# A two-layer decoder step: raw inputs to the projections, gates and cached values in another order

## What is computed

```
xn = x * rsqrt(mean(x*x) + eps) * norm_attn            # the factor rsqrt(...) is one number per token
u, q, k, v, gates = split(xn @ w_in)                   # 512 + 3*1536 + 2048 columns
q, k = rmsnorm per head of q, k
pool_o = mixer of running means of u;  att_o = three attention groups, prompt and cached keys and values
x += (sigmoid(g0) * (pool_o @ w_bp) + sigmoid(g1) * (att_o @ w_ba)) @ w_out
x += FFN(rmsnorm(x))           # layer 0: dense SwiGLU; layer 1: top 2 of 8 experts
```

## Time and profile before

| what | value |
|---|---|
| median of three runs | 1980.35 us |
| the profiled execution itself | 1980.97 us |
| its span, first to last instruction | 1979.2 us |
| TensorE busy | 1900.2 us (96%) |
| VectorE, ScalarE, POOL busy | 621.4, 466.5, 165.1 us |
| mean granted TensorE clock | 0.985 |
| moved by DMA | 553.81 MB, 280 GB/s |

### The profile page before, as it was taken

How to read it: one execution, slowest core, us unless ns; L and a number is a source line. 1 busy time by engine, 2 the same in 40 slices (tenths; PEclk the granted TensorE clock), 3 DMA queues, 4 the chain that set the end, 5 groups by cost and what they waited for, 6 DMA issues and landing times.

```text
span 1979.2 us, 44750 instructions
## 1 busy us (share of the span) xinstructions
PE 1900.2 (96%) x20521; PEld 1305.5 (66%) x20522; DVE 621.4 (31%) x1037; ACT 466.5 (24%) x708; POOL 165.1 (8%) x239
## 2 busy tenths in 40 slices
PE   6999988999999999998899999999999999999998
PEld 5998876999999999886786353443535353443534
DVE  4455631554444445641353101020101102020101
ACT  3444432344433444532232100000000000000000
POOL 0113100113321011400010000000000000000000
PEclk8999999999999999999998999999999999999999
DMA  7443688745545444388935999999999999999996
GB/s 235 158 143 126 216 281 303 244 129 170 169 162 169 136 151 153 124 277 275 312 103 191 350 408 380 412 374 416 387 403 406 382 409 379 412 375 415 393 398 267
DMA packets 211901, 553.81 MB, mean 280 GB/s; under 512 B 11402, under 2 KB 107706, under 8 KB 195056
## 3 DMA queue, kind: packets, MB, share of 16 engines
q1 hardware_dynamic: 207184, 541.67, 74.1%
q0 software_dynamic: 3248, 9.18, 1.3%
q10 hardware_dynamic: 1280, 0.06, 0.1%
HBM read 543.46 MB, written 7.77 MB: 279 GB/s over the span
## 4 chain that ended last, share of the span: by engine, by line
PE 91%; DMA 3%; DVE 3%; ACT 2%; issue 1%; POOL 0%; SPq 0%; DVEq 0%; ACTq 0%; POOLq 0%
PE psum L906 86%; PE psum L914 5%; DMA low_part<-in_w_in 3%; DVE w_split L1739 1%; ACT w_split L1470 1%; DMA high_part<-in_const_a 0%; DVE high_part L1746 0%; DVE low_part L2201 0%; DVE low_part L1732 0%; DVE low_part L1834 0%; ACT high_part L1447 0%; DVE high_part L1839 0%; ACT low_part L1443 0%; POOL high_part L2357 0%; DVE high_part L1732 0%
## 5 line engine op out<-in xcount | busy, mean ns | idle before, releaser
L906 PE MATMUL psum<-low_part 128*32 128x512 f32 (+3 forms) x6926 | 672.0, 526 | 6.8 <-ACT low_part L1443 4.7
L906 PE MATMUL psum<-xn_split,w_split 128*128 128x288 f32 x3744 | 530.3, 302 | 37.7 <-DVE w_split L1739 21.9
L906 PEld LDWEIGHTS psum<-xn_split,w_split 128*128 128x128 f32 x3744 | 515.3, 193 | 62.8 <-DVE w_split L1739 35.4
L906 PEld LDWEIGHTS psum<-low_part 128*32 128x32 f32 (+2 forms) x6926 | 241.4, 114 | 405.1 <-issue 397.3
L1739 DVE TENSOR_TENSOR w_split<-low_part,w_split 128x2048 fp32r<-128x2048 f32 x105 | 240.9, 2294 | 367.6 <-ACT w_split L1470 367.5
L906 PE MATMUL psum<-low_part,high_part 128*32 128x256 f32 (+3 forms) x6636 | 345.1, 359 | 3.9 <-DVE low_part L1732 2.4
L906 PEld LDWEIGHTS psum<-low_part,high_part 128*32 128x32 f32 (+1 forms) x6636 | 218.5, 111 | 130.0 <-issue 15.6
L1470 ACT ACTIVATE w_split<-low_part 128x2048 fp32r<-128x2048 f32 x105 | 200.9, 1914 | 366.7 <-PE psum L906 230.8
L2213 DVE TENSOR_TENSOR low_part<-high_part,psum 128x384 f32<-128x384 f32 (+1 forms) x48 | 29.8, 621 | 426.2 <-PE psum L906 423.8
L914 PE MATMUL psum<-high_part,low_part 128*128 128x128 f32 (+2 forms) x839 | 107.7, 278 | 12.5 <-DMA high_part<-in_const_a 9.4
L1703 ACT ACTIVATE high_part<-psum 128x384 f32<-128x384 f32 (+1 forms) x48 | 25.9, 544 | 395.0 <-PE psum L906 394.1
(11 more groups left out here) (153 smaller groups left out, 919.5 us busy)
## 6 DMA issues: line engine op xcount, KB each, us to landing
low_part<-in_we_down SPq DMA_DIRECT2D x112, 1024.0 KB, 8.4
low_part<-in_cache_kv_g SPq DMA_DIRECT2D x72, 1024.0 KB, 5.6
low_part<-in_we_gate SPq DMA_DIRECT2D x64, 1024.0 KB, 8.0
low_part<-in_we_up SPq DMA_DIRECT2D x64, 1024.0 KB, 8.4
low_part<-in_w_in SPq DMA_DIRECT2D x56, 1024.0 KB, 5.1
low_part<-in_we_gate SPq DMA_DIRECT2D x64, 768.0 KB, 7.4
low_part<-in_we_up SPq DMA_DIRECT2D x64, 768.0 KB, 6.8
low_part<-in_w_dense SPq DMA_DIRECT2D x33, 1024.0 KB, 5.2
```

Of the source, the lines that this page charges most:

```text
L906: signal(e.matmul(out, lhsT, rhs, start=start, stop=stop, skip_group_check=mixed), inc)
```

## The change

- **Factor behind the projections.** In both layers the attention norm's projections take raw x times the gain: ScalarE makes its high part (`raw_high`), VectorE its low part (`raw_low`). `rstd` is multiplied when u, v and gate tiles are evicted, on VectorE now; q and k need it only in the epsilon of their own norm, for which VectorE adds eps * rms^2 to the sums (head sums). v tiles and gates were evicted on ScalarE before; ScalarE now takes the sigmoid from SBUF.
- **Squares.** POOL adds the eight squared tiles, and one sum-of-squares product with ones remains per norm. It stands after the second z tile (attention), or after the first FFN tile.
- **Start.** SP sends the identity, then the inputs and the first weight chunk in halves, chunks 1 to 4, and then the rest of the table. Transposes, copies, splits and the first two u tiles go by halves of the features.
- **Layer 1's start.** The last FFN chunk runs column by column, its sums in banks 4 to 7 and 0 to 3; VectorE makes a low part after each column that it adds.
- **FFN.** Its second chunk is split ahead of root and reciprocal.
- **Gate stage.** Value chunks follow each half of a gate chunk, and gates 1 to 7 are loaded one value chunk earlier than they are used (`value_loads`). The second head gather comes after the last gate, and the first two pool branch tiles before the attention ones (`branch_tiles`).
- **Evictions.** v tiles are evicted ahead of the weight split of the same step on VectorE.

```
-V_BEHIND = (2, 3, 3, 3, 3, 2, 2, 0)
+V_BEHIND = ((1, 1), (1, 1), (2, 1), (1, 1), (2, 1), (1, 1), (1, 1), (2, 0))
 
 
 def value_steps():
 
     out, v = [], 0
-    for gate, n in enumerate(V_BEHIND):
-        out.append(("G", gate))
-        out += [("V", v + i) for i in range(n)]
-        v += n
+    for gate, behind in enumerate(V_BEHIND):
+        for x, n in enumerate(behind):
+            out.append(("G", gate, x))
+            out += [("V", v + i, 0) for i in range(n)]
+            v += n
     return out
 
 
 V_STEPS = value_steps()
 
 
+def value_loads():
+
+    out = [(kind, n) for kind, n, x in V_STEPS if x == 0]
+    for gate in range(1, KT):
+        i = out.index(("G", gate))
+        if out[i - 1][0] == "V":
+            out[i - 1], out[i] = out[i], out[i - 1]
+    return out
+
+
+V_LOADS = value_loads()
...
+    js = [(("x", tt, 0), None) for tt in range(3)] + [(("gain", 0), None)]
+    return js + [(("x", tt, 1), None) for tt in range(3)]
...
-    js = [(("ssq", 0), None)]
-    js += [(("u", c), None) for c in range(PG)]
+    js = [(("u", c), (4, 5, 6, 7)) for c in range(PG)]
     for n in range(36):
+        if n == 2:
+            js.append((("ssq", 0), (3,)))
...
-    return js + [(("fd", c), None) for c in range(KT)]
+    return js + [(("fd", c), ((c + 4) % KT,)) for c in range(KT)]
...
+            e.dma_start(ident, io["const_a"][:, 0:PART]).then_inc(ident_loaded, 16)
+            def columns(w, a):
+                return w.rearrange("(k p) n -> p k n", p=PART)[:, :, a:a + 256]
+
+            for hf in range(2):
+                for tt, (a, n) in enumerate(TT):
+                    src = io["x_prompt"][0, a:a + n, :] if tt < 2 else io["x_sample"].rearrange("b t d -> (b t) d")
+                    half = slice(D // 2 * hf, D // 2 * (hf + 1))
+                    e.dma_start(x_raw[0:n, tt, half], src[:, half]).then_inc(x_loaded[hf], 16)
+                k = slice(KT // 2 * hf, KT // 2 * (hf + 1))
+                e.dma_start(view(slot(0), KT, 256)[:, k], columns(io["w_in"][0], 0)[:, k])\
+                    .then_inc(loaded[0] if hf else half_loaded, 16)
...
-                for kind, n in V_STEPS:
+                for kind, n in V_LOADS:
...
-                for k in range(KT):
-                    e.wait_ge(sq_ready.sem, sq_ready.at(L, 8 * i + k + 1))
-                    mm(S.ps(("ssq", i))[:, 0:T], ones, work[:, k, :], k == 0, k == KT - 1,
-                       full[S.bank(("ssq", i))] if k == KT - 1 else None)
-
-            def ssq_tile(L, S, k):
-
-                if k == 0:
-                    S.wait_free(e, ("ssq", 1))
-                e.wait_ge(sq_ready.sem, sq_ready.at(L, 8 + k + 1))
-                mm(S.ps(("ssq", 1))[:, 0:T], ones, work[:, k, :], k == 0, k == KT - 1,
-                   full[S.bank(("ssq", 1))] if k == KT - 1 else None)
+                e.wait_ge(sq_sum.sem, sq_sum.at(L, (KT - 1) * (i + 1)))
+                mm(S.ps(("ssq", i))[:, 0:T], ones, work[:, 0, :], True, True, full[S.bank(("ssq", i))])
...
+            for hf in range(2):
+                e.wait_ge(x_loaded[hf], 48)
...
+                    w = held.rearrange("p a (k n) -> p a k n", k=KT)
+                    for h in range(2):
+                        if (L, h) == (0, 1):
+                            e.wait_ge(lo_ready, 1)
+                        for c in range(2):
+                            job = ("u", c)
+                            if h == 0:
+                                S.wait_free(e, job)
+                            for k in range(KT // 2 * h, KT // 2 * (h + 1)):
+                                if c == 0:
+                                    e.wait_ge(xl_ready.sem, xl_ready.at(L, k + 1))
+                                mm3(S.ps(job)[:, 0:T], [w[:, a, k, 128 * c:128 * (c + 1)] for a in range(2)],
+                                    [x[:, k, :] for x in xn_parts], k == 0, k == KT - 1,
+                                    full[S.bank(job)] if k == KT - 1 else None)
+                    done.append(split_used)
...
+                    if n == 2:
+                        ssq(L, S, 0)
...
-                def gates(n):
+                def gates(n, x):
                     w = chunk(L, W_MERGE + n).rearrange("p a (k n) -> p a k n", k=KT)
-                    for x in range(2):
-                        project(S, (f"g{n % 2}", n // 2 * 2 + x), lambda a, k: w[:, a, k, 128 * x:128 * (x + 1)], xn_parts)
-                        if (n, x) == (KT - 1, 0):
-                            gather_heads(1)
-                    done.append(split_used)
-
-                for kind, n in V_STEPS:
+                    project(S, (f"g{n % 2}", n // 2 * 2 + x), lambda a, k: w[:, a, k, 128 * x:128 * (x + 1)], xn_parts)
+                    if x == 1:
+                        done.append(split_used)
...
+                for kind, n, x in V_STEPS:
                     if kind == "V":
                         cache_values(n)
                         continue
-                    gates(n)
-                    if n == 0:
+                    gates(n, x)
+                    if (n, x) == (0, 1):
                         turn_s_probs(1)
-                    elif n == EX0_GATE:
+                    elif (n, x) == (EX0_GATE, 1):
                         gather_heads(0)
+                    elif (n, x) == (KT - 1, 1):
+                        gather_heads(1)
...
-                    if c >= 1 and L == 0:
-                        ssq_tile(0, dense_sec, c - 1)
...
-                                ssq_tile(0, S, KT - 1)
+                                ssq(0, S, 1)
...
+                    if i < FT // 2 - 1:
+                        for f in (2 * i, 2 * i + 1):
+                            e.wait_ge(hl_ready, f + 1)
+                            for n in range(KT):
+                                down(w, f, n)
+                    else:
+                        e.wait_ge(hl_ready, FT)
+                        for n in range(KT):
+                            for f in (2 * i, 2 * i + 1):
...
+            def raw_high(L, k):
+
+                e.activation(xn_split[:, 0, k, :], xT[:, k, :], ACT.Copy, scale=gain[:, k:k + 1]).then_inc(xh_ready.sem, 1)
...
+                        turned_x(1, hf)
+                        if hf == 1:
+                            turned_x(2, 1)
+                        first_halves(hf)
+                        for tt in range(3):
+                            pre.wait_read(e, ("x", tt, hf))
+                        if hf == 0:
+                            e.wait_ge(gain_ready.sem, gain_ready.at(0, 1))
+                        for k in range(4 * hf, 4 * hf + 4):
+                            raw_high(0, k)
+                else:
+                    e.wait_ge(gain_ready.sem, gain_ready.at(1, 1))
+                    for k in range(KT):
+                        dense_sec.wait_read(e, ("fd", k))
+                        raw_high(1, k)
+                split_high(L, 1)
+                for k in range(KT):
+                    e.activation(work[:, k, :], xT[:, k, :], ACT.Square).then_inc(sq_ready.sem, 1)
+                split_high(L, 2)
+                split_high(L, 3)
+                root(S, 0)
...
-                    elif c >= 24:
-                        v = c - 24
-                        copy(S, ("zv", v), vT[v // 4][:, v % 4, :], S.ps(("zv", v))[:, 0:T])
...
-                        S.freed(e.activation(gate[2 * job[1] + n % 2], S.ps(job)[:, 0:T], ACT.Sigmoid), job)
-                        if (n, x) == (KT - 1, 0):
+                        g = gate[2 * job[1] + n % 2]
+                        e.wait_ge(gate_scaled.sem, gate_scaled.at(L, 2 * n + x + 1))
+                        e.activation(g, g, ACT.Sigmoid).then_inc(gate_ready.sem, 1)
...
-                norm(0, S, 1, W_UP + 1)
+                split_high(0, W_UP + 1)
+                root(S, 1)
...
-                for k in range(KT + 1 if i == 0 else 0):
-                    if k < KT:
-                        e.scalar_tensor_tensor(out=xn[:, k, :], in0=xT[:, k, :], scalar=gain[:, 8 * i + k:8 * i + k + 1],
-                                               in1=rstd, op0=ALU.mult, op1=ALU.mult).then_inc(xn_ready.sem, 1)
-                    if k >= 1:
-                        e.wait_ge(xh_ready.sem, xh_ready.at(L, 8 * i + k))
-                        e.tensor_tensor(xn_split[:, 1, k - 1, :], xn[:, k - 1, :], xn_split[:, 0, k - 1, :].bitcast(F32),
-                                        ALU.subtract).then_inc(xl_ready.sem, 1)
...
+            def raw_low(L, i, k):
+
+                e.wait_ge(xh_ready.sem, xh_ready.at(L, KT * i + k + 1))
+                g = gain[:, KT * i + k:KT * i + k + 1]
+                e.scalar_tensor_tensor(out=xn_split[:, 1, k, :], in0=xT[:, k, :], scalar=g, in1=xn_split[:, 0, k, :].bitcast(F32),
+                                       op0=ALU.mult, op1=ALU.subtract).then_inc(xl_ready.sem, 1)
...
+            turned_x(0, 0)
+            turned_x(2, 0)
```

(83 more changed lines are left out.)

206 lines of the change are left out of this document (106 added, 100 removed).

## The result

The changed kernel takes 1924.16 us (median of 4 runs, 1921.44 to 1929.35) against 1979.8 us in the same rounds: a ratio of 0.9726 with a 95% interval of 0.9699 to 0.9752. The forecast was 1918.8 us, with a range of 1904 to 1941. The profiled execution took 1922.89 us, its span is 1921.0.

A forecast was written before the change was run, and what follows sets the result against it. TensorE, busy 96% of the span, was taken as the bound, so time is won at its waits, lower clock or removable work. Gains 17.8 + 9.6 + 6.2 + 28.0 = 61.6 us gave 1918.8 us, range 1904 to 1941.

The forecast's parts named there:

- Start of layer 0: Program start: first projection at 12.0 us, u done at 26.2 with the later sum of squares against 44.04; gain 17.8 us.
- the rest, costed at nothing: Value evictions on VectorE, POOL's additions, the table's later sending and chunk 5 behind it: no cost; MoE untouched.
- Late gains: Rival at layer 0's start: gains land with the router's weights, start gains 12.9 us, time 1923.7; chance 0.15.
- Layer 1's start: Last FFN chunk by columns: u3 ends at 651.8 against 661.90, new stall of 1.8 before u2; gain 9.6 us.
- Squares: Seven square products at 0.47 us move to POOL, and waits of 1.14 and 1.82 go; gain 6.2 us.
- Gates: Both layers' gate stages: 80.5 and 81.4 us, transfers bounding next, TensorE's floor 77.2; gain 14.8 + 13.2 = 28.0 us.
- 13.7 against 14.2: Gate stage: 13.7 us of work from gate 3's load to its use against 14.2 of transfer and split; just fits.
- four waits of 12.3: Layer 0's old gate stage: four TensorE waits for the load-and-split loop of gate weights come to 12.3 us.
- Transfers keep the stage: Rival in the gate stage: saturated transfers only reordered, late values replace late gates; time 1946.8; chance 0.17.
- The lower clock takes it: Rival in the gate stage: waits make gate halves run at 1.2 GHz, stage 130.6 us, time 2018; chance 0.03.
- A factor that stays on the path: Rival: z4 waits for u0's bank behind POOL's late sums, both layers wait some 5 us; time 1929; chance 0.10.
- Value tiles at nothing: Value tiles' evictions move from ScalarE to VectorE at about the same length, costing nothing as VectorE is at 31%.

The follow-up runs named there:

- e2: Changed kernel with the rest of the table sent behind chunk 2, ahead of chunks 3 and 4: 1918.74 us, ratio 0.9698.
- e11: Changed kernel with the table sent behind chunk 2 and also awaited only at its first use: 1920.19 us, ratio 0.9698.
- e12: Changed kernel run again with no edit, on the same chip: 1925.52 us, ratio 0.9726.
- e7: Changed kernel with the last FFN chunk run row by row again: 1926.59 us, ratio 0.9723.
- e8: Changed kernel with eight square products with ones on TensorE again, POOL adding nothing: 1935.22 us, ratio 0.9774.
- e6: Changed kernel with gates made of one product in place of three, all transfers kept: 1918.21 us, one run.
- e4: Changed kernel with the old order of use in the gate stage, but the new earlier gate loads: 1934.17 us, ratio 0.9775.
- e5: Changed kernel with the new order of use in the gate stage, but loads in the order of use: 1939.05 us, ratio 0.9797.
- e9: Changed kernel with value tiles evicted behind the weight split of the same step on VectorE: 1933.62 us, ratio 0.9777.

## Why the prediction was right, and where it wasn't

- **Start of layer 0: the mechanism right, one term missed.** First projection forecast at 12.0, measured 12.61; u done at 25.7, measured 26.67. The step that failed stands under "the rest, costed at nothing": the table's remainder "wanted only by z tiles". z0 begins the moment u is done, the wait stands before z0 and not before the first product that reads the table, and 1,000 KB behind four chunks landed at 30.7. Cost: 4.03 of wait and 1.5 of slower tiles; e2 and e11 get 5.3 us back. The trace of the kernel before had a price for it: a chunk of 1 MB issued in its first 20 us took 14.1 us to landing (median of six), where the median of all chunks of this weight is 5.1.

```profile
low_part<-in_w_in SPq DMA_DIRECT2D x6, 1024.0 KB, 14.1
```

- **The sum: in part luck.** The 5.3 us happen to be the whole distance from 1918.8 to 1924.2. In the profiled execution the start fell 6.25 short and gates, branches and experts 1.7; 4.5 came that the forecast didn't have: 1.0 in w_out and FFN, 2.0 in layer 1's start, 1.5 in the last stage but one. The last two are within what executions of the same kernel differ by (e12). The 1.0 fits a slow piece of the kernel before, a granted clock of 0.72 from 430 to 436 us behind the wait of 1.82.
- **Late gains (0.15): no.** Thirteen of the first matmuls ran in one piece from 5.31, the gains' transpose being the last of them. The Trainium skill (DMA: Bandwidth & Descriptors, Queues, rings and completion order) has a DMA engine take turns between queues packet by packet. The prediction set its late end, 12.9 in place of 17.8, beside that rule; here the small loads were in time beside SP's queue, so the rule didn't decide.
- **Layer 1's start: right.** Forecast 14.9 us from the FFN's end to u's end, measured 14.3; the new stall before u2 forecast at 1.8, measured 1.29. e7 shows that 2.3 of the gain hang on the order by columns.
- **Squares: right.** 0.47 each forecast, 0.48 in e8; the two waits of the earlier trace rows are gone. No run takes back the sums' place or the FFN's early split alone, so what each of the two waits was worth rests on the timelines.
- **Gates: the size right, the bound wrong.** 80.5 and 81.4 were forecast with "the transfers as what bounds next" and a floor of 77.2 for TensorE. Measured were 81.8 and 81.5, but e6 puts the transfers at 75.7 or less and e2 TensorE at 79.7. The failed step is the reading of share times length (0.84 of 95.3) as pure transfer. The floor was 2.5 short; seven pairs of gate halves that came in one piece before, at 0.18 more, and twelve single value steps, at 0.06 or more, make about 2 of it. The two stages of the profiled execution hold 1.8 and 1.4 us more than e12's (79.99 and 80.14), at a clock of 0.98. The chain "13.7 against 14.2" did fit, with the work nearer 14.1 by the steps measured, and e4 and e5 show that it takes both orders. Of the four waits of 12.3 that the prediction took for turns of the loop, one of 2.4 ends with a copy on VectorE (L1732) and not with a split.
- **Transfers keep the stage (0.17): no**, though e4 shows a late value in the late gate's place once the order of use stays old. **The lower clock takes it (0.03): no**; the granted clock rose from 0.93 and 0.95 to 0.98.
- **A factor that stays on the path (0.10): no.** POOL's last addition ended at 28.24, ten us before the product that reads it, and no z tile waited for u's bank. No run puts the factor back ahead of the projections: what it gives at the two starts rests on the timelines before and after.
- **Value tiles at nothing: right for a wrong reason.** The cover isn't a VectorE that is busy 31%, it is the place ahead of the split: 8.1 to 9.5 us (e9).

## What to carry to other kernels

A wait belongs at the first instruction that reads what it waits for, and a load that is "wanted only later" has to be costed from the bytes queued ahead of it. Where two streams share a ring of buffers, try the order of use and the order of loads separately and together: here each alone gave about half, and under the old order of use the earlier loads of one stream made the other wait. An engine's low share hides nothing by itself; the place of an instruction in that engine's queue does.

## What the runs showed that was not expected

- An issue on SP that takes 0.4 us elsewhere takes far longer at the start: four chunks 9.37 us and the table 5.48 (SP's rows above), with three to seven transfers of SP under way. The number under way isn't enough to explain it: the 278 issues of the changed kernel that find three under way have a median of 0.34. Whether the long issue delays anything by itself isn't shown: from 12.61 to 26.68 us the transfers run at 347 GB/s, at a DMA share of 1.09, so the bytes ahead may be all of it.
- POOL's additions of equal size (288 columns) took 0.79 to 2.93 us:

```profile
L2409 POOL TENSOR_TENSOR high_part<-high_part x7: 789/809/2927, 18.2 to 27.5; 128x288 f32<-128x288 f32 x7
```

The two long ones, 2.24 from 18.20 and 2.93 from 22.50, began beside the weight splits of VectorE at 17.48 and 22.46 (2.29 each). Of all 21 additions of the profiled execution, the seven over 1 us ran beside a weight split. The Trainium skill (GPSIMD Engine Reference, Specifications) says that GpSimd shares its SBUF interfaces with VectorE and contends with instructions there that have two SBUF inputs. A weight split has two, and the rows agree. It isn't always GpSimd that pays: beside the addition at 379.90, which kept its 0.81, VectorE's low part of x (L1836, two inputs as well) took 0.74 where it takes 0.51.
- Pieces at the lower clock come and go between executions of one kernel, some without a wait of TensorE before them (granted clock 0.72 from 303 to 309 us of the profiled execution, TensorE busy all the while): the first gate stage took 81.79 in one execution and 79.99 in another (e12), and the stretch up to the expert stage 74.3 or 76.0. Stages of single executions are to be compared with 2 us of doubt.
